# Grid attention: one unit of each head in turns on the array's halves, four PT buffers

## The reference

```python
q = qk_norm(q, q_gain) * HEAD_DIM ** -0.5      # RMS norm over the head's 64 values
k = qk_norm(k, k_gain)
# all 8 rows are keys for every query; 16 columns round the query's own
s = einsum('qd,kd->qk', q, k) + bias            # bias by row and column offset
s = where(col_mask, s, NEG_INF)
prob = softmax(s)
out = einsum('qk,kd->qd', prob, v)
```

## Time and profile before

| | us |
|---|---|
| median of 3 runs (lowest, highest) | 2456.04 (2454.46, 2462.33) |
| the profiled execution | 2464.16 |
| its span, first to last instruction | 2462.0 |
| grid attention, first product to last take_out | 1328.5 to 1507.4 |
| PE busy in the whole span | 2204.4 (90%) |
| DVE, ACT, POOL busy | 1008.2, 791.5, 876.9 |
| mean granted TensorE clock | 0.949 of full |

### The profile page before, as it was taken

The page is one execution under the profiler, slowest core; times in us unless marked ns, Lnnn a source line. Parts: engine busy times, 40 slices in busy tenths (PEclk is TensorE's granted clock), DMA queues, the critical chain, the costliest instruction groups (busy, mean ns, idle before and its releaser), DMA issues. The chain is left out here.

```text
span 2462.0 us, 29987 instructions
## 1 busy us (share of the span) xinstructions
PE 2204.4 (90%) x11405; PEld 1693.9 (69%) x11405; DVE 1008.2 (41%) x1671; ACT 791.5 (32%) x1248; POOL 876.9 (36%) x787
## 2 busy tenths in 40 slices
PE   6999898999988988999996997899999988599994
PEld 5888776777876776888885665677877767344441
DVE  4122255667662454223335554335546345311112
ACT  4333242344332434323324443422222143111110
POOL 3433046665662444444421111254354333000001
PEclk9999989999999999999997999898899999699997
DMA  4423032233322443332314312221121243799994
GB/s 146 127 71 93 4 110 71 75 90 96 86 59 77 133 147 105 102 102 85 102 52 82 73 61 65 64 52 27 48 48 27 80 147 131 310 408 422 424 423 172
DMA packets 290326, 307.61 MB, mean 125 GB/s; under 512 B 78384, under 2 KB 248624, under 8 KB 280560
## 3 DMA queue, kind: packets, MB, share of 16 engines
q1 hardware_dynamic: 281464, 274.14, 34.9%
q0 software_dynamic: 5280, 19.18, 2.1%
q10 hardware_dynamic: 3456, 12.58, 1.2%
HBM read 325.67 MB, written 30.51 MB: 145 GB/s over the span
## 5 line engine op out<-in xcount | busy, mean ns | idle before, releaser
L2405 PE MATMUL moe_bank<-ex_wgu,Y 128*64 128x512 f32 x768 | 171.2, 597 | 1.6 <-ACT Y L2452 1.6
L655 PE MATMUL gdn_bank<-hh,gdn_ws 128*128 128x512 f32 x368 | 161.2, 438 | 9.6 <-POOL gdn_ws L885 9.6
L885 POOL TENSOR_TENSOR gdn_ws<-gdn_wr,gdn_ws 128x1024 fp32r<-128x1024 f32 x44 | 105.6, 2404 | 116.8 <-ACT gdn_ws L1179 116.8
L657 PE MATMUL gdn_bank<-hh,gdn_ws 128*128 128x512 f32 x368 | 146.0, 397 | 0.0
L656 PE MATMUL gdn_bank<-hl,gdn_ws 128*128 128x512 f32 x368 | 145.3, 395 | 0.0
L2405 PEld LDWEIGHTS moe_bank<-ex_wgu,Y 128*64 128x64 f32 x768 | 66.2, 138 | 101.1 <-issue 101.1
L2377 POOL DMA_INDIRECT hT<-token_rows,rows x24 | 22.9, 953 | 301.4 <-PE moe_bank L2390 236.5
L2083 DVE TENSOR_TENSOR ff_hes<-hT,ff_hes 128x1024 fp32r<-128x1024 f32 x16 | 23.4, 1460 | 207.5 <-ACT ff_hes L2042 207.5
L3094 POOL TENSOR_TENSOR rw_ws<-rw_wr,rw_ws 128x1024 fp32r<-128x1024 f32 x27 | 64.4, 2387 | 121.6 <-ACT rw_ws L3485 121.6
L655 PE MATMUL rw_bank<-hh,rw_ws 128*128 128x512 f32 x232 | 102.7, 443 | 5.2 <-POOL rw_ws L3094 5.2
L655 PE MATMUL ff_bank<-ff_wds,ff_hes 128*128 128x512 f32 x256 | 99.7, 390 | 1.8 <-DVE Y L2099 1.8
(11 more groups left out here) (578 smaller groups left out, 5772.6 us busy)
## 6 DMA issues: line engine op xcount, KB each, us to landing
ex_wgu<-in_w_gate_e SPq DMA_DIRECT2D x48, 1024.0 KB, 15.9
ex_wgu<-in_w_up_e SPq DMA_DIRECT2D x48, 1024.0 KB, 21.6
ex_wd<-in_w_down_e SPq DMA_DIRECT2D x48, 1024.0 KB, 20.7
Y<-in_w_in SPq DMA_DIRECT2D x48, 512.0 KB, 3.9
gdn_wr<-in_w_in SPq DMA_DIRECT2D x44, 512.0 KB, 4.2
wu<-in_w_ff SPq DMA_DIRECT2D x16, 1024.0 KB, 11.2
ff_wd<-in_w_ff SPq DMA_DIRECT2D x16, 1024.0 KB
rw_wr<-in_w_in SPq DMA_DIRECT2D x27, 512.0 KB
```

The lines of the kernel that those rows point to most:

```text
L655: pe.matmul(bank, left(0, l), right(0, r), start=(start and n == 0), stop=False)
L657: ins = pe.matmul(bank, left(1, l), right(0, r), start=False, stop=(stop and n == len(pairs) - 1))
L885: pool.tensor_tensor(ws[:, r % 2, 1], raw[r], ws[:, r % 2, 0], ALU.subtract).then_inc(s.lo, 1)
L2405: ins = pe.matmul(bank[2 + j][half, :], hgT[:, j, k, half], w[:, e, k], start=(k == 0), stop=(k == KT - 1))
```

## The change

Units are numbered anew: `unit(a)` gives the pair a // 8, the head a % 2, and the block a % 8 // 2, so that units 2n and 2n+1 are the same block of the two heads. PE works them together. Logits are no longer one matmul over 128 rows with zeros, but two matmuls of 256 columns over the head's own 64 rows, the two heads in turns, into two banks. Values go chunk by chunk, the two heads in turns, at their own 64 columns of the array. qz with its zeroing becomes qT. PT has four buffers. PE's loop makes four double steps instead of eight steps, and `fill` and `squares` are placed anew; the orders on ACT and DVE stay.

```diff
-        qz = ph.sb("qz", [P, 2, 2, T])
+        qT = ph.sb("qT", [P, 2, T])
...
-        PT = ph.sb("PT", [P, 2, T])
+        PT = ph.sb("PT", [P, 4, T])
...
+        def unit(a):
+
+            return a // UNITS, a % 2, a % UNITS // 2
+
+        def own(e):
+            return slice(64 * e, 64 * e + 64)
...
             def logits(a):
...
-                if a >= 3:
-                    pe.wait_ge(s.taken, a - 2)
-                pe.matmul(bank[2 + a % 3][:, :], qz[:, i % 2, e, t * P:(t + 1) * P], kT[:, i % 2, :],
-                          start=True, stop=True).then_inc(s.logits, 1)
+                if a >= 2:
+                    pe.wait_ge(s.taken, a - 1)
+                for half in range(2):
+                    c0 = slice(half * 256, half * 256 + 256)
+                    for e in range(2):
+                        ins = pe.matmul(bank[2 + (a + e) % 3][:, c0], qT[own(e), i % 2, t * P:(t + 1) * P], kT[own(e), i % 2, c0], start=True, stop=True)
+                        if half:
+                            ins.then_inc(s.logits, 1)
...
             def values(a):
-                i, e, t = a // UNITS, a % UNITS // 4, a % 4
-                pe.wait_ge(s.pt, a + 1)
+                i, _, t = unit(a)
+                pe.wait_ge(s.pt, a + 2)
...
                 for n in range(NT):
-                    ins = pe.matmul(bank[7][64 * e:64 * e + 64, t * P:(t + 1) * P], v[:, i % 2, n, 64 * e:64 * e + 64],
-                                    PT[:, a % 2, n * P:(n + 1) * P], start=(n == 0), stop=(n == NT - 1))
-                ins.then_inc(s.out, 1)
+                    for e in range(2):
+                        ins = pe.matmul(bank[7][own(e), t * P:(t + 1) * P], v[:, i % 2, n, own(e)],
+                                        PT[:, (a + e) % 4, n * P:(n + 1) * P], start=(n == 0), stop=(n == NT - 1))
+                        if n == NT - 1:
+                            ins.then_inc(s.out, 1)
...
-            for a in range(3):
-                logits(a)
+            logits(0)
+            logits(2)
             turn(0)
+            turn(1)
             for i in range(PAIR):
...
-                for m in range(UNITS):
+                for m in range(0, UNITS, 2):
                     a = UNITS * i + m
                     if more and m == 2:
                         squares(i + 1, 0)
+                    if more and m == 4:
+                        squares(i + 1, 1)
                     if more and m == 6:
                         turn_v(i + 1)
-                    fill((3, 3, 3, 2, 2, 0, 0, 0)[m])
-                    turn(a + 1)
-                    logits(a + 3)
-                    fill((3, 2, 2, 2, 2, 0, 0, 0)[m])
-                    if more and m == 3:
-                        squares(i + 1, 1)
+                    logits(a + 4)
+                    fill((4, 4, 2, 0)[m // 2])
+                    turn(a + 2)
+                    fill((4, 3, 2, 0)[m // 2])
+                    turn(a + 3)
+                    fill((3, 2, 0, 0)[m // 2])
                     values(a)
...
             def turn(a):
                 act.wait_ge(s.turned, a + 1)
-                if a >= 2:
-                    act.wait_ge(s.out, a - 1)
-                act.activation(PT[:, a % 2, :], bank[5 + a % 2][:, :], ACT.Copy).then_inc(s.pt, 1)
+                if a >= 4:
+                    act.wait_ge(s.out, a - 3)
+                act.activation(PT[:, a % 4, :], bank[5 + a % 2][:, :], ACT.Copy).then_inc(s.pt, 1)
...
-                for e in range(2):
-                    own = slice(64 * e, 64 * e + 64)
-                    ins = dve.scalar_tensor_tensor(dst[own, e], src[own], gn[own, 0:1], by[own], ALU.mult, ALU.mult)
-                ins.then_inc(s.qk, 1)
+                dve.scalar_tensor_tensor(dst, src[:, :, ::-1], gn[:, 0:1], by[:, :, ::-1], ALU.mult, ALU.mult).then_inc(s.qk, 1)
...
-            c.link(dve.memset(qz[:], 0.0))
```

More of the change, by code:

```diff
@@ L2803, in unit_q @@
                 dve.wait_ge(s.rn, 2 * i + 1)
-                dst = qz[:, i % 2].rearrange("p e (r c) -> p e r c", c=NAROW)
-                src, by = (a.rearrange("p (r c) -> p r c", c=NAROW)[:, :, ::-1] for a in (raw[:, 0, :], rn[:, 0, :]))
+                dst, src, by = (a.rearrange("p (r c) -> p r c", c=NAROW) for a in (qT[:, i % 2, :], raw[:, 0, :], rn[:, 0, :]))
                 if i >= 2:
                     dve.wait_ge(s.logits, UNITS * (i - 1))
-                for e in range(2):
-                    own = slice(64 * e, 64 * e + 64)
-                    ins = dve.scalar_tensor_tensor(dst[own, e], src[own], gn[own, 0:1], by[own], ALU.mult, ALU.mult)
-                ins.then_inc(s.qk, 1)
+                dve.scalar_tensor_tensor(dst, src[:, :, ::-1], gn[:, 0:1], by[:, :, ::-1], ALU.mult, ALU.mult).then_inc(s.qk, 1)
             def unit_k(i):
@@ L2824, in masked @@
                     return
-                i, e, t, r = a // UNITS, a % UNITS // 4, a % 4, a % 4
+                (i, e, t), r = unit(a), a % 4
                 if a % UNITS == 0:
```

## The result

The changed kernel takes 2500.34 us (median; 2498.9 to 2505.47), the kernel before 2456.04. The ratio on record is 1.0148, 95% interval 1.0108 to 1.0187; the quotient of the two medians, 1.0180, lies inside it. Forecast were 2493 us and "slower". The profiled execution took 2498.9 us, its span is 2497.1 us against 2462.0. The gap of the medians, 44.3 us, is larger than the 34.7 between the two profiled executions because the one of before lies 8.1 us above its own median and the one of after 1.4 us under its own. Unrounded that is +35.4 where the prediction's sum said +36.5, and it is the whole difference of the spans (35.1).

The account below looks back on a forecast made before the run. PE sets the pace while projection chunks fill; after the change it waits on ACT's order before turns. Stalls, less savings, give +19.5 us at full clock, clock falls 17: 36.5 over 2456, so 2493 us, range 2468 to 2512.

Parts of the forecast that it names:

- L pair: Two units' logits on PE, in alternating row halves: 1.09 us, was 1.72.
- V pair: Two units' values on PE, in alternating column halves: 1.2 us, was 2.4.
- The rivals in which halves don't pair: PE's array: column halves not side by side, +13, 2506 us, chance 0.03; neither half pairs, +21, 2514 us, chance 0.02.
- A: PE's wait before the turn of unit 3, whose exponential stands behind the copy of q: 5.2 us.
- B: PE's wait before the turn of unit 5, behind the copy of k, two chunks lying over it: 3.8 us.
- C: Logits of the next heads wait on PE for k, directly behind the squares they need: 2.35 us.
- D: PE's wait before the turn of unit 7, behind the copy of v, which has no square: 4.5 us.
- E: PE's wait before the turn of unit 8, behind turn_v, its copy, exponential and scaling: 1.3 us.
- F: PE's wait before the turn of unit 9, for DVE's mask and scaling: 1.7 us.
- the collision: DVE's scaling starts inside POOL's split, freed by `higher`, and takes 1.19 us instead of 0.49.
- so a period is 50.3 us: One filled period of grid attention, with stalls summing to 18.85 us: 50.3 us against 41.1, at full clock, taken three times.
- the tail: The last units, from the turn of unit 25 to the last `take_out`: 17.85 us, was 23.55, a gain of 5.7.

Follow-up runs that it names:

- old_order_pairs: The changed kernel's paired matmuls in the step order of the kernel before (fills, turns and squares where they were): 2433.74 us, ratio 0.9895.
- rows_alone: The kernel before, with each unit's logits as one matmul over the head's own 64 rows and 512 columns, by itself: 2480.39 us, ratio 1.0075.
- pool_late: The changed kernel, but POOL's split waits until the DVE scaling it would run beside is done: 2484.49 us, ratio 1.0091.
- higher_late: The changed kernel, but ACT runs `higher` one exponential later: 2472.99 us, ratio 1.0051.
- squares_early: The changed kernel, but the next pair's squares of k go a step earlier, behind turn(a+3): 2492.05 us, ratio 1.011.
- values_first: The changed kernel, but values(a) and the step's third fill go ahead of turn(a+3) instead of behind it: 2462.6 us, ratio 1.0001.
- kept_busy: The changed kernel, but PE runs 1 to 5 spare matmuls ahead of the turns of units 3, 5 and 7: 2481.28 us, ratio 1.0096.
- combined: The changed kernel with values before turn(a+3), `higher` one exponential later and the squares of k two chunks before the logits: 2439.12 us, ratio 0.9906.
- old_order_higher_late: The changed kernel's pairs in the step order of the kernel before, with `higher` one exponential later on ACT: 2428.7 us, ratio 0.9866.

## Why the prediction held

**What PE gains: right.** L pair 1.06 us to the next start (1.09 forecast); V pair 1.02 (the 1.2 forecast held both changes of shape). In old_order_pairs a period of PE's work is 32.3 us against the 31.5 of the sum; before it was 38.8 by the same sum and 39.0 busy. The Trainium skill's rule that weight loads overlap running matmuls only when the row group differs (TensorE: Matmul & The Clock Gate, "The mechanism") does not describe these column halves: the prediction's estimate by it was 2.05 us, measured were 1.02, and 1.52 without turns between the halves. The rivals in which halves don't pair are out, and rows_alone shows the pairing itself, not the shorter contraction, to be what pays.

**What PE then waits for: right, one by one.** Forecast and measured in the first period: A 5.2 and 5.00; B 3.8 and 3.62; C 2.35 and 2.23; D 4.5 and 4.34; E 1.3 and 0.61 (1.04 in the later periods); F 1.7 and 1.44. pool_late and higher_late take the parts out singly, 1.28 for the collision and 0.95 for `higher`, and squares_early C; values_first shows that the place of the values and fills alone takes A from 5.00 to 1.74. That the cover went, and not that the work grew, is thereby shown.

**The clock: the sum right, the places only in part.** In the first period it was 0.57 over 4 us behind A and B and 0.60 behind D, as sized (1.7 us each), and held behind C. Later it differed (windows of 4 us behind B in the second period, behind C in the third, and behind F at T9):

```profile
1444.90:1448.90 4.00, 3.99 (x28) 2.59 (x28) 0.00 (x0) 0.00 (x0) 0.00 (x0) 1.00 0.64 204
1503.50:1507.50 4.00, 3.97 (x15) 2.79 (x16) 3.41 (x8) 0.38 (x1) 0.00 (x0) 0.62 0.00 0
1412.20:1416.20 4.00, 4.00 (x28) 3.16 (x28) 0.93 (x2) 0.80 (x3) 0.00 (x0) 0.57 0.16 20
```

B's same 3.62 us brought no fall there, C's 2.23 us was followed by one, and so was F's 1.44; behind A in the second period the clock was down for longer (0.57 over 1425.00 to 1433.00). From T1 to T25 it was 0.88, up to 162.1 x 0.12 = 19 us lost for the 17 forecast. That the wrong places evened out is luck. Periods one and two were 56.05 and 55.93 us against 55.9 and 55.4 forecast (three falls each; the first lacks a V and has the start's 1.7).

**Two mistakes cancelled.** The third period took 50.1 us, not 55.4. It has no next weights to prepare for k and v, so `higher` is missing before T21 and T23 and nothing collides; their waits in the timeline:

```profile
1497.18 0.66 PE L2686 MATMUL na_bank<-const,Y 128*128 128x128 f32 x4 [1.40 <-DVE Y L2855]
...
1511.74 0.66 PE L2686 MATMUL na_bank<-const,Y 128*128 128x128 f32 x4 [2.10 <-DVE Y L2855]
```

2.2 us less than B and D, each the same 0.95 + 1.28 as in higher_late. The step that failed is "so a period is 50.3 us", taken three times although the weights of the last pair end one period earlier: 4.4 us too much. Against it stands the tail: 21.12 us from T25 to the last `take_out` and not 17.85. It was worked out at full clock, and the granted clock was 0.76 over it, up to 21.1 x 0.24 = 5.1 us. Inside the periods the prediction gave a fall only to stalls of 3.8 us or more, and none to the tail. kept_busy (round T8 and T9), rows_alone and the change itself at T9 and T25 show falls where PE's waits just before were 1.5 us and less; what exactly decides in such a stretch stays open. Before, the same tail with waits of 1.34 us kept its clock.

**The start: 2.5 us off** in place, T1 at 1356.15 for 1358.6; the phase began 2.7 us earlier, so its length up to T1 was as forecast (30.4 and 30.1 us).

**From the sum to the median.** The profiled difference came within 1.8 us (34.7 for 36.5). The median came 7 us over 2493 because of what was carried over: the profiled execution of before was 8.1 us above its median, and the time outside the phase doesn't repeat better than that: in the thirteen profiles it lies between 2273.8 and 2289.6 us.

**What stays open.** Why row halves run side by side in either order, and column halves gain 0.5 us from taking turns. What decides the clock in stretches of turns, pairs and short waits is open as well. Nothing large is hidden outside the phase: from the phases alone the ratios would be 1.0144 for the change, 0.9903 for combined, 0.9885 for old_order_pairs and 0.987 for old_order_higher_late (its 32.1 us of 2460.45), and the ratios on record are 1.0148, 0.9906, 0.9895 and 0.9866.

## What to carry to other kernels

A faster inner operation shortens the work that lay over someone else's chain: before work is grouped in larger units, list for each wait what stands between its last producer and the waiting instruction in the new order, since here the pairs saved 7 us of work a period and their order brought 17 us of waits, while the same pairs in the old order made the phase 28 us shorter than before. Prepare what is needed later (here `higher`) behind what is needed now, on the in-order engine that feeds the ring; three calls moved by one place were worth 22 us. And price a stall on TensorE with the clock behind it.

## What the runs showed of the hardware

- A scaling on DVE that starts inside POOL's split ends 0.3 us after it (0.49 us becomes 1.19 in the earlier trace rows and 1.77 here), and the reverse holds: in pool_late the split, started 0.23 us into a DVE addition of 2.02 us, took 4.02 us and not 2.34. What was left of the addition, 1.79, plus 2.34 is 4.13. The Trainium skill (SBUF — State Buffer, "Terms") says that one of the two engines holds a shared port pair for a whole instruction and the other blocks; both rows agree to about 0.2 us.
- Two float32 matmul groups of 64 rows run side by side: 1.06 us a pair in turns, 1.07 one after the other, 1.05 for one alone with as many columns. For 64-column halves it is 1.02 in turns and 1.52 not.
- A float32 matmul over half the rows between ones over all of them cost 0.09 us ahead, 0.19 in itself and 0.11 behind.
- In the change the granted clock fell with each wait of 5.00 us and behind both of 4.33 and 4.34, behind one wait of 3.62 us and not behind the next of 3.62, behind one of the three of 2.23, and behind two of the three of 1.44 us. One length of wait on PE did not decide it.
